# GpSimd forms the column units of a modulation matrix ahead, and the weight ring has seven slots, in a two-layer hybrid encoder

## Chip, cores, metric

One core of a Trainium2 chip runs the whole program in one launch. The metric is the device time in microseconds, median of the runs.

## What is computed

Two layers over x (512 tokens of 1024 channels, float32). Every layer first forms six modulation vectors from the conditioning vector c, then runs four groups of token mixers side by side and a mixture of 32 experts:

```python
ca = jax.nn.silu(c)
for l in range(DEPTH):
    mod = ca @ w_ada[l] + b_ada[l]
    sh1, sc1, gt1, sh2, sc2, gt2 = [m[:, None, :] for m in jnp.split(mod, 6, axis=-1)]
    h = rms_norm(x, g_norm1[l]) * (1.0 + sc1) + sh1
    proj = h @ w_in[l]
    # ya, yb, yc, yd: differential attention, neighbourhood attention, convolution, dilated attention
    mix = jnp.concatenate([ya, yb, yc, yd], axis=-1) @ w_out[l]
    x = x + gt1 * mix
    h2 = rms_norm(x, g_norm2[l]) * (1.0 + sc2) + sh2
    x = x + gt2 * hier_moe(h2, w_router_group[l], w_router_expert[l],
                           w_exp_gate[l], w_exp_up[l], w_exp_down[l])
return rms_norm(x, g_final)
```

w_ada is 1024 x 6144 per layer. Each of the 32 experts has three matrices of 2 MB; a token uses two experts of one group of eight.

## The kernel before

The weights come in units of 2 MB (128 partitions x 8 x 512; some are 1 MB) into a ring of six slots, loaded by SyncE in the order of the list ORDER. SyncE works strictly in that order: before each load it waits until the slot's earlier unit has been used. w_ada of a layer is twelve such units of 512 columns (u = 0 to 11): 0 and 1 are the first shift, 2 and 3 the first scale, 4 and 5 the first gate, 6 to 9 the second shift and scale, 10 and 11 the second gate.

- ADA_EARLY, the gates (4, 5, 10, 11): VectorE multiplies and adds them during the projections (early_product), TensorE sums over the partitions and spreads the result.
- ADA_LATER, the column units 6 to 9: in the attention, at steps 1, 9, 12 and 29 (ADA_STEPS). TensorE multiplies the silu vector with the unit (ada, L1041), which gives a row. VectorE turns it into columns (ada_turned, L1768), and two steps later (MOD_LAG) TensorE folds it (mod, L1059) and VectorE adds the bias (mod_out).
- ADA_NEXT, the units 0 to 3 of layer 1, are done in the same way in the routing of layer 0, between the last router logits and the first expert.

A layer goes through these stages. The projections go group by group, D, A, B, with q and k first, then v (product, L1015). In them VectorE rotates q and k and runs the 31 taps of the convolution over 2 x 128 channels (tap, L1793); the last 31 of 62 tap instructions stand in one piece ahead of B's first q and k. The attention has 32 units in 35 steps: D at 0 to 7, A at 8 to 23, B at 24 to 31. In a step i TensorE turns the probabilities of an earlier unit (turn, L1184), makes the scores of unit i (scores, L1170) and the output of another (attend, L1197 and L1210). VectorE takes maxima, ScalarE takes exponentials (expo, L1581 and L1584) and copies the turned probabilities out of PSUM (prob_out, L1598). Odd pairs are copied into z, the buffer of the convolution. So the first of these copies waits for conv_ready, which GpSimd gives when it has copied the convolution's result from z to yT (L930).

GpSimd's queue in a layer is: small loads (L917 to L921), those two copies, the bias tables of B's first two heads (L936 to L945, once D's last scores are used, since they lie over D's q and k), the tables of the other two (once A's last scores are used), six additions x += tmp in the output projection (L952), and then the gathers and scatters of the experts (L970, L980).

The output projection (out_part, L1228) is followed tile by tile by the transposes and logits of the router. Routing then ranks the tokens. In layer 1, which has no next units, idle_products (L1071) stand in the places of the row products.

The experts take their weights from nine places of 2 MB, three experts' worth: the six slots, home (a buffer used by nothing else), hT and work. BUF sets their order, await_first_free what the first load of each waits for (L843). After that each half place is loaded again as soon as TensorE has used it (expert_unit, L864). In layer 0 the order is home, then the places of the two w_out units, hT, the four slots of the ADA_NEXT units and work.

## Time and profile before

| | |
|---|---|
| median of 3 runs | 1806.28 us (1804.26 to 1807.28) |
| profiled execution | 1805.69 us |
| its span, first to last instruction | 1803.8 us |
| TensorE busy | 1589.4 us, 88% |
| VectorE, ScalarE, GpSimd busy | 39%, 24%, 11% |
| HBM | 520.99 MB read, 302 GB/s over the span |

Stages of the profiled execution, in us from the start of the span: layer 0 has its projections up to 208, the attention up to 312, the output projection up to 381, routing up to 411 and the experts up to 891. Layer 1 starts at 918, its attention at 1087, its output projection at 1192, routing at 1261, the experts at 1287, and they end at 1775. "Idle before" in a row is the time that the engine stood before the instruction, and behind the arrow stands what ended it. TensorE's counts are twice those of the program's text, since each float32 product is two records. L numbers are lines of the kernel above.

### The profile page before, as it was taken

The numbers are of one execution on the slowest core, as the hardware profiler recorded it, in microseconds if no ns is written. First come the engines' busy times: TensorE is split into PE (matmuls) and PEld (weight loads), VectorE is DVE, ScalarE is ACT, GpSimd is POOL, SyncE is SP. The second block draws the span as 40 slices with busy tenths as digits, with TensorE's granted clock in tenths as the row PEclk, the third lists the DMA queues.
The fourth block names the chain that finished last, engine by engine and source line by source line (L and its number), as shares of the span: only waits on it lengthen the run. The fifth ranks groups of instructions, "written<-read, shape, count | busy, mean of one in ns | idle before, by whom it ended". The sixth has DMA issues, their size and how long they took to land.

```text
span 1803.8 us, 22591 instructions
## 1 busy us (share of the span) xinstructions
PE 1589.4 (88%) x7494; PEld 763.4 (42%) x7494; DVE 695.3 (39%) x1432; ACT 435.6 (24%) x989; POOL 194.1 (11%) x199
## 2 busy tenths in 40 slices
PE   5999998998998998787889999999899988887883
PEld 2455645453333343333345555455333333333331
DVE  1677576352222112222157855743422222222124
ACT  2111567112111112111121016742111221111111
POOL 0000022111111011111000002101111111111010
PEclk9999999989999999999999999999999999999997
DMA  9625533079999999999972355212799999999994
GB/s 362 231 70 202 195 115 110 17 293 398 407 401 407 408 408 404 417 410 417 365 298 93 122 204 208 68 48 101 290 400 407 403 409 406 411 416 404 399 395 180
DMA packets 118493, 527.56 MB, mean 292 GB/s; under 512 B 16529, under 2 KB 22673, under 8 KB 69265
## 3 DMA queue, kind: packets, MB, share of 16 engines
q1 hardware_dynamic: 100944, 491.49, 69.0%
q0 software_dynamic: 12496, 24.51, 4.2%
q10 hardware_dynamic: 4976, 10.55, 1.6%
q8 instruction: 46, 0.75, 0.2%
q14 instruction: 31, 0.25, 0.0%
HBM read 520.99 MB, written 23.86 MB: 302 GB/s over the span
## 4 chain that ended last, share of the span: by engine, by line
PE 56%; DMA 27%; SPq 6%; DVE 5%; issue 3%; ACT 3%; POOL 1%; ACTq 0%; DVEq 0%; POOLq 0%
DMA ring<-in_w_exp_up 20%; PE ps L1015 18%; PE ps L1373 17%; PE ps L1228 6%; SPq L841 5%; PE ps L1371 4%; DMA hT<-in_w_exp_up 3%; PE ps L1170 2%; PE ps L1184 2%; PE ps L1210 2%; PE ps L1041 1%; DMA ring<-in_w_in 1%; ACT arena L1664 1%; DMA yexp_d<-arena,masks 1%; PE ps L1404 1%
## 5 line engine op out<-in xcount | busy, mean ns | idle before, releaser
L1373 PE MATMUL ps<-ring,arena 128*64 128x512 f32 x1952 | 589.1, 603 | 59.2 <-ACT arena L1664 35.0
L1373 PEld LDWEIGHTS ps<-ring,arena 128*64 128x64 f32 x1952 | 184.8, 138 | 273.5 <-issue 260.2
L1015 PE MATMUL ps<-ring,hT 128*128 128x512 f32 (+1 forms) x768 | 255.0, 487 | 1.5 <-DVE z L1804 0.9
L733 DVE TENSOR_TENSOR arena<-ps,arena 64x512 f32<-64x512 f32 (+1 forms) x64 | 44.3, 693 | 488.6 <-ACT arena L1658 418.6
L1658 ACT ACTIVATE arena<-ps 128x512 f32<-128x512 f32 x64 | 38.2, 597 | 778.9 <-PE ps L1373 724.3
L1015 PEld LDWEIGHTS ps<-ring,hT 128*128 128x128 f32 x768 | 144.4, 191 | 101.5 <-issue 91.2
L1373 PE MATMUL ps<-home,arena 128*64 128x512 f32 x320 | 148.6, 619 | 24.2 <-DMA ring<-in_w_exp_up 20.5
L1373 PE MATMUL ps<-hT,arena 128*64 128x512 f32 x336 | 151.5, 605 | 6.9 <-DMA ring<-in_w_exp_up 6.9
L980 POOL DMA_INDIRECT yexp_d<-arena,masks x64 | 59.3, 927 | 850.3 <-DVE arena L743 772.9
L741 DVE TENSOR_TENSOR arena<-ps,gate 64x512 f32<-64x512 f32 (+1 forms) x64 | 43.7, 683 | 266.2 <-PE ps L1373 246.6
L1228 PE MATMUL ps<-ring,hT 128*128 128x512 f32 x256 | 112.5, 595 | 0.0
L1650 ACT ACTIVATE arena<-ps,modc 128x128 f32<-128x128 f32 x256 | 96.5, 457 | 32.3 <-PE ps L1352 30.1
L1373 PEld LDWEIGHTS ps<-home,arena 128*64 128x64 f32 x320 | 44.6, 143 | 118.9 <-issue 116.9
L1793 DVE SCALAR_TENSOR_TENSOR work<-z,small,work 128x512 f32<-128x512 f32 x120 | 90.0, 751 | 3.9
L722 DVE TENSOR_SCALAR arena<-ps,modc 128x128 f32<-128x128 f32 x256 | 87.4, 403 | 5.9 <-PE ps L1352 2.3
L1373 PE MATMUL ps<-work,arena 128*64 128x512 f32 x320 | 73.1, 598 | 17.9 <-ACT arena L1664 17.9
L1352 PEld LDWEIGHTS ps<-cst,arena 128*128 128x128 f32 x512 | 62.2, 194 | 51.7 <-issue 51.7
L1352 PE MATMUL ps<-cst,arena 128*128 128x128 f32 x512 | 73.7, 287 | 2.4 <-DVEq L1759 2.4
L1170 PE MATMUL ps<-arena 64*128 64x512 f32 (+1 forms) x256 | 73.7, 655 | 0.0
L1228 PEld LDWEIGHTS ps<-ring,hT 128*128 128x128 f32 x256 | 47.8, 190 | 57.1 <-issue 57.1
L1373 PEld LDWEIGHTS ps<-hT,arena 128*64 128x64 f32 x336 | 45.8, 139 | 57.1 <-issue 56.0
L1404 PE MATMUL ps<-cst,arena 128*128 128x128 f32 x256 | 47.8, 309 | 23.9 <-DVE arena L733 23.7
(218 smaller groups left out, 1645.2 us busy)
## 6 DMA issues: line engine op xcount, KB each, us to landing
ring<-in_w_exp_up SPq DMA_DIRECT2D x108, 1024.0 KB
ring<-in_w_exp_down SPq DMA_DIRECT2D x88, 1024.0 KB
ring<-in_w_exp_gate SPq DMA_DIRECT2D x62, 1024.0 KB
ring<-in_w_ada SPq DMA_DIRECT2D x24, 2048.0 KB, 11.1
home<-in_w_exp_gate SPq DMA_DIRECT2D x44, 1024.0 KB
work<-in_w_exp_down SPq DMA_DIRECT2D x40, 1024.0 KB
hT<-in_w_exp_gate SPq DMA_DIRECT2D x22, 1024.0 KB
hT<-in_w_exp_up SPq DMA_DIRECT2D x20, 1024.0 KB
```

The source lines that it names most:

```text
L722: last = dve.tensor_scalar(xgT[j][:, k, :], ps[:, 4, P * q:P * q + P], modc[:, 3, k:k + 1], modc[:, 2, k:k + 1], ALU.mult, ALU.add)
L841: sp.dma_start(places[b][:, n * h:n * h + n], flat[i % SPAN][e][:, n * h:n * h + n]).then_inc(half_in[h][b], 16)
L980: pool.indirect_dma_start(yexp_d[l], bass.IndirectOffsetOnAxis(ap=lst[0:w, e:e + 1], axis=0), yexp[e % 2][0:w, :], None, bounds_check=last ...
L1015: last = pe.matmul(out, lhs(k), rhs(k), start=(k == 0), stop=(k == n - 1))
L1170: fills(pe.matmul(bank(key), qkT[g][p0:p0 + n, hp, P * t:P * t + P], qkT[g][p0:p0 + n, 2 + hp, :], start=True, stop=True, tile_position=(p ...
L1228: last = pe.matmul(bank(key), yT[:, k, P * t:P * t + P], slot(unit)[:, k, :], start=(k == K_OUT[0]), stop=(k == K_OUT[-1]))
L1352: last = pe.transpose(bank_e(b).rearrange("p (a s) -> p a s", a=4)[:, q, :], xg[j][:, k:D:KD], ident)
L1371: last = [pe.matmul(outs[c], lhs(k), rhs(c, k), start=(k == 0), stop=(k == n - 1)) for c in range(2)]
L1373: last = [pe.matmul(outs[c][HALF * c:HALF * c + HALF, :], lhs(k)[:, 0:HALF], rhs(c, k), start=(k == 0), stop=(k == n - 1), tile_position=( ...
L1404: last = pe.transpose(ps[:, 2, P * c:P * c + P], hid[j][:, c:DE:KE], ident)
L1650: last = act.activation(xgT[j][:, q, :], ps[:, 3, P * q:P * q + P], ACT.Identity, scale=modc[:, 3, q:q + 1], bias=modc[:, 2, q:q + 1])
L1793: ins = dve.scalar_tensor_tensor(conv[f], z[:, f, k:k + S], w, conv[f], ALU.mult, ALU.add)
```

## The change

Three things.

1. ADA_LATER and ADA_NEXT units are formed on GpSimd (column_sums): one multiplication of the whole unit, in its ring slot, by the silu vector, and three instructions that add its eight parts to one. TensorE then sums over the partitions with eight products of a single column (mod_of_sums), and VectorE adds the bias as before. The row product, its turning and its copy are gone for these units; units 0 to 3 of layer 0 stay as they were.
2. Places: GpSimd does the four later units ahead of the copies of the convolution, the first unit of layer 1 behind them, two more between the two pairs of bias tables, and the last behind the tables. TensorE's sums stand at steps 4, 8, 10, 12 (later) and 16, 23, 27 and output tile 2 (next). Routing has none left, and its idle products now run in both layers.
3. home is gone and the ring has seven slots. The experts still have nine places; in layer 0 the five slots of the last later unit and the four next units come first, then w_out's two, hT and work.

```diff
-SLOTS = 6
+SLOTS = 7
-ADA_STEPS = [1, 9, 12, 29]
+LATER_STEPS, NEXT_STEPS, NEXT_TILE = [4, 8, 10, 12], [16, 23, 27], 2
-MOD_LAG = 2
+def mods_at(l, step):
+    later = [ADA_LATER[l][n] for n, s in enumerate(LATER_STEPS) if s == step]
+    return later + [unit for unit, s in zip(ADA_NEXT[l], NEXT_STEPS) if s == step]
...
-        order += [("ada",) + item for item in ADA_LATER[l]]
+        order += [("ada",) + item for item in ADA_LATER[l] + ADA_NEXT[l][:1]]
         order += [("wout", l, n) for n in range(2)]
-        order += [("ada",) + item for item in ADA_NEXT[l]]
+        order += [("ada",) + item for item in ADA_NEXT[l][1:]]
...
         if ADA_NEXT[l]:
-            last = [HOME] + late[0:2] + [FEATURES] + late[2:6] + [WORK]
-        else:
-            last = [HOME] + late + [FEATURES, WORK]
+            late = late[0:2] + late[4:] + late[2:4]
+        last = late + [FEATURES, WORK]
...
-        home = sb("home", [P, KD, 512])
...
-                if old is not None:
+                if old is not None and ORDER[old][0] == "ada" and ORDER[old][1:] in ADA_EARLY[l]:
+                    sp.wait_ge(early_ready, len(ADA_EARLY[l]) * l + ADA_EARLY[l].index(ORDER[old][1:]) + 1)
+                elif old is not None:
                     await_filled(sp, last_use(old))
...
                     if b == WORK:
                         sp.wait_ge(slots_ready, 2 * l + 2)
-                        if not ADA_NEXT[l]:
-                            sp.wait_ge(xg_in[0], 16 * (l * HE + 1))
-                        for m, u in ADA_NEXT[l][-1:]:
-                            await_filled(sp, (m, "mod", u))
+                        sp.wait_ge(xg_in[0], 16 * (l * HE + 1))
...
+                def column_sums(m, u):
+                    unit = UNIT["ada", m, u]
+                    await_unit(pool, unit)
+                    w = slot(unit)
+                    link(pool.tensor_tensor(w, w, view(csil, 0, [[KD, P], [1, KD], [0, 512]]), ALU.mult))
+                    for n in (4, 2):
+                        link(pool.tensor_tensor(w[:, 0:n, :], w[:, 0:n, :], w[:, n:2 * n, :], ALU.add))
+                    pool.tensor_tensor(w[:, 0, :], w[:, 0, :], w[:, 1, :], ALU.add).then_inc(sums_ready, 1)
+                pool.wait_ge(silu_ready, 1)
+                for m, u in ADA_LATER[l]:
+                    column_sums(m, u)
                 await_filled(pool, (l, "v", "B", TT - 1))
                 for f in range(2):
                     pool.wait_ge(conv_silu, 2 * l + f + 1)
                     pool.tensor_copy(yT[:, FIRST_F["C"] + f, :], z[:, f, HALO:HALO + S]).then_inc(conv_ready, 1)
+                for m, u in ADA_NEXT[l][:1]:
+                    column_sums(m, u)
                 for hp in range(2):
...
+                    for m, u in ADA_NEXT[l][1 + 2 * hp:3 + 2 * hp]:
+                        column_sums(m, u)
...
+            def mod_of_sums(l, u):
+                key, w, p0 = (l, "mod", u), slot(UNIT["ada", l, u]), HALF * (u % 2)
+                pe.wait_ge(sums_ready, sums_before(l, u) + 1)
+                await_free(pe, key)
+                for k in range(KD):
+                    last = pe.matmul(bank(key)[p0:p0 + HALF, k:k + 1], w[:, 0, k:512:KD], C["ones"],
+                                     start=True, stop=True, tile_position=(0, p0))
+                fills(last, key)
...
-                    if ada_at(l, i - MOD_LAG) is not None:
-                        n = ada_at(l, i - MOD_LAG)
-                        mod(*ADA_LATER[l][n], n % 2)
+                    for m, u in mods_at(l, i):
+                        mod_of_sums(m, u)
                     for u in closed_at(i):
                         attend(u)
-                    if ada_at(l, i) is not None:
-                        ada(*ADA_LATER[l][ada_at(l, i)])
```

On TensorE this is the start of layer 0's attention before, from the scores of the first two steps on; L1041 is the row product of step 1, L1059 its fold at step 3:

```order
49 L1170 MATMUL ps<-arena 128x512 x4
50 L1041 MATMUL ps<-ring,csil 32x512 x8
51 L1184 MATMUL ps<-cst,work 128x128 x8
52 L1170 MATMUL ps<-arena 128x512 x2
53 L1184 MATMUL ps<-cst,work 128x128 x8
54 L1170 MATMUL ps<-arena 128x512 x2
55 L1059 MATMUL ps<-work,cst 32x8 x2
56 L1197 MATMUL ps<-cst,rinv 64x128 x2
57 L1210 MATMUL ps<-work,arena 64x128 x8
```

And now, where L1055 is the new sum over the partitions (the other lines are the same instructions, moved by ten or eleven lines of text):

```order
49 L1181 MATMUL ps<-arena 128x512 x4
50 L1195 MATMUL ps<-cst,work 128x128 x8
51 L1181 MATMUL ps<-arena 128x512 x2
52 L1195 MATMUL ps<-cst,work 128x128 x8
53 L1181 MATMUL ps<-arena 128x512 x2
54 L1208 MATMUL ps<-cst,rinv 64x128 x2
55 L1221 MATMUL ps<-work,arena 64x128 x8
56 L1195 MATMUL ps<-cst,work 128x128 x8
57 L1181 MATMUL ps<-arena 128x512 x2
58 L1055 MATMUL ps<-cst,ring 64x1 x8
```

The row product has gone from step 1, and one step behind the place of its fold, at step 4, stand eight products of one column, read from the ring.

On GpSimd the queue of layer 0 before, from the last small load to the first tables:

```order
13 L921 DMA masks<-in_dilation 128x896
14 L930 COPY hT<-z 128x512 [waits bank_filled2,conv_silu,table_in,params_in]
15 L930 COPY hT<-z 128x512 [waits conv_silu]
16 L936 DMA arena<-in_rpb 64x896 [waits bank_drained3]
17 L936 DMA arena<-in_rpb 64x896 x3
```

And now (rows 19 to 30 are three more units like rows 15 to 18):

```order
15 L919 TENSOR_TENSOR ring<-ring,csil 128x4096 [waits silu_ready,slot_in1,table_in,params_in]
16 L921 TENSOR_TENSOR ring<-ring 128x2048 [waits pool_chain]
17 L921 TENSOR_TENSOR ring<-ring 128x1024 [waits pool_chain]
18 L922 TENSOR_TENSOR ring<-ring 128x512 [waits pool_chain]
...
31 L930 COPY hT<-z 128x512 [waits conv_silu,bank_filled2]
32 L930 COPY hT<-z 128x512 [waits conv_silu]
33 L919 TENSOR_TENSOR ring<-ring,csil 128x4096 [waits slot_in5]
...
37 L938 DMA arena<-in_rpb 64x896 [waits bank_drained3]
...
43 L919 TENSOR_TENSOR ring<-ring,csil 128x4096 [waits slot_in1]
...
51 L938 DMA arena<-in_rpb 64x896 [waits bank_drained3]
```

The copies and both pairs of tables now stand behind whole units, and each unit behind the load of its slot.

## Rows read from the trace of the kernel before

**Rows 1.** Stage windows: stretch, length, busy and instructions of PE, PEld, DVE, ACT, POOL, clock, DMA, GB/s

```profile
411.00:891.00 480.00, 419.15 (x1892) 173.46 (x1892) 105.92 (x217) 83.95 (x187) 55.54 (x59) 0.99 1.01 406
1287.00:1775.00 488.00, 416.38 (x1912) 169.45 (x1912) 107.16 (x218) 86.13 (x190) 56.40 (x60) 0.98 0.98 392
312.00:381.00 69.00, 68.92 (x265) 36.33 (x266) 22.05 (x34) 12.73 (x26) 7.54 (x6) 1.00 0.21 78
```

**Rows 2.** The page's part 4, chain of waits by line, share of the span

```profile
DMA ring<-in_w_exp_up 20%; PE ps L1015 18%; PE ps L1373 17%; PE ps L1228 6%; SPq L841 5%; PE ps L1371 4%; DMA hT<-in_w_exp_up 3%; PE ps L1170 2%; PE ps L1184 2%; PE ps L1210 2%; PE ps L1041 1%; DMA ring<-in_w_in 1%; ACT arena L1664 1%; DMA yexp_d<-arena,masks 1%; PE ps L1404 1%
```

**Rows 3.** TensorE in the attention: timeline (start, us), then windows of 5 us

```profile
209.16 1.92 PE L1041 MATMUL ps<-ring,csil 128*32 128x512 f32 x16
247.63 3.64 PE L1041 MATMUL ps<-ring,csil 128*32 128x512 f32 x16
...
240.00:245.00 5.00, 3.66 (x36) 1.00 0.80 270
245.00:250.00 5.00, 4.82 (x20) 0.59 0.41 155
```

**Rows 4.** Timeline of TensorE, from the last logits to the first expert, both layers

```profile
381.16 3.66 PE L1015 MATMUL ps<-arena,hT 128*128 128x36 f32 x32
...
392.22 3.55 PE L1064 MATMUL ps<-cst,work 128*64 128x1 f32 x32
...
411.24 1.08 PE L1373 MATMUL ps<-home,arena 128*64 128x512 f32 x1 [1.81 <-ACT arena L1650]
...
1260.62 3.66 PE L1015 MATMUL ps<-arena,hT 128*128 128x36 f32 x32
...
1287.02 0.61 PE L1373 MATMUL ps<-home,arena 128*64 128x512 f32 x1 [1.81 <-issue]
```

**Rows 5.** Timeline of ScalarE in layer 0's attention: first copy to z, exponentials of steps

```profile
215.71 1.06 ACT L1598 ACTIVATE z<-ps 128x512 f32<-128x512 f32 x2
...
234.31 0.69 ACT L1581 ACTIVATE work<-ps,masks 128x512 f32<-128x512 f32 x1 [0.96 <-DVE masks L1901]
...
263.29 0.69 ACT L1581 ACTIVATE arena<-ps,masks 128x512 f32<-128x512 f32 x1
...
265.74 0.69 ACT L1581 ACTIVATE work<-ps,masks 128x512 f32<-128x512 f32 x1 [0.52 <-DVE masks L1901]
```

**Rows 6.** Groups of GpSimd by form: busy, mean ns, idle before

```profile
L952 POOL TENSOR_TENSOR x<-x,work 128x512 f32<-128x512 f32 x12 | 15.1, 1265 | 118.8 <-DVE work L1998 118.8
L945 POOL TENSOR_TENSOR arena<-arena,cst 128x896 f32<-128x896 f32 x8 | 14.3, 1787 | 0.7
```

**Rows 7.** Timeline of SyncE's queue, and a load's median from issue to landing

```profile
144.65 30.54 SPq L796 DMA_DIRECT2D ring<-in_w_ada  x4
...
ring<-in_w_out SPq DMA_DIRECT2D x4, 2048.0 KB, 7.8
```

**Rows 8.** Timeline of GpSimd in layer 0's attention

```profile
208.49 0.61 POOL L930 COPY hT<-z 128x512 f32<-128x512 f32 x1 [0.32 <-ACT z L1567]
231.60 2.12 POOL L936 DMA_DIRECT2D arena<-in_rpb  x4 [22.50 <-DVE masks L1914]
...
281.95 2.17 POOL L936 DMA_DIRECT2D arena<-in_rpb  x4 [35.17 <-ACT work L1581]
...
295.15 1.77 POOL L945 TENSOR_TENSOR arena<-arena,cst 128x896 f32<-128x896 f32 x1
```

**Rows 9.** Windows up to 13 us behind the first expert, layers 0 and 1

```profile
361.00:424.00 63.00, 55.85 (x315) 31.36 (x313) 30.45 (x115) 13.16 (x26) 7.07 (x6) 0.86 0.83 319
1237.00:1300.00 63.00, 55.54 (x257) 31.12 (x257) 27.78 (x105) 12.08 (x24) 7.67 (x7) 0.97 0.60 220
```

**Rows 10.** Timelines: VectorE's taps; GpSimd's and VectorE's instructions that overlap

```profile
145.35 24.24 DVE L1793 SCALAR_TENSOR_TENSOR work<-z,small,work 128x512 f32<-128x512 f32 x31
...
238.01 2.46 POOL L944 TENSOR_SCALAR arena<-arena 128x896 f32<-128x896 f32 x1 [4.29 <-DMA arena<-in_rpb]
...
240.01 0.75 DVE L1932 SCALAR_TENSOR_TENSOR work<-work,coef 128x512 f32<-128x512 f32 x1
```

More of the change, by code:

```diff
@@ L115, with sums_before @@
 ADA_NEXT = [[(l + 1, u) for u in range(NORM1_UNITS) if l + 1 < DEPTH] for l in range(DEPTH)]
-def ada_at(l, step):
-    return ADA_STEPS.index(step) if step in ADA_STEPS else None
+def mods_at(l, step):
+    later = [ADA_LATER[l][n] for n, s in enumerate(LATER_STEPS) if s == step]
+    return later + [unit for unit, s in zip(ADA_NEXT[l], NEXT_STEPS) if s == step]
+def sums_before(m, u):
+    order = [unit for l in range(DEPTH) for unit in ADA_LATER[l] + ADA_NEXT[l]]
+    return order.index((m, u))
 def unit_order():
@@ L153, in plan_buffers @@
         else:
-            left = [last[n] for n in (6, 7, 1, 4, 2, 5, 0, 3, 8)]
-            order = [b for b in left if b < SLOTS]
+            order = [last[n] for n in (6, 7, 8, 0, 1, 3, 4, 2, 5) if last[n] < SLOTS]
         ring.append({n: order[i % SLOTS] for i, n in enumerate(ATT[l])})
@@ L253, in plan_banks @@
         for step in range(NSTEP):
-            if ada_at(l, step - MOD_LAG) is not None:
-                m, u = ADA_LATER[l][ada_at(l, step - MOD_LAG)]
+            for m, u in mods_at(l, step):
                 take((m, "mod", u), 7)
@@ L261, in plan_banks @@
                     take((l, "meanA", f), (7, 3)[f])
-            if ada_at(l, step) is not None:
-                m, u = ADA_LATER[l][ada_at(l, step)]
-                take((m, "ada", u), 7)
         for t in range(TT + 1):
@@ L270, in plan_banks @@
                 take((l, "router_shift"), 7)
+            if t == NEXT_TILE:
+                for m, u in ADA_NEXT[l][len(NEXT_STEPS):]:
+                    take((m, "mod", u), 7)
             if t:
@@ L497, in last_use @@
             if kind == "ada":
-                return l, "mod" if (l, u) in ADA_EARLY[l] else "ada", u
+                return l, "ada" if l == 0 and u < NORM1_UNITS else "mod", u
             if kind == "win":
@@ L843, in await_first_free @@
                 def await_first_free(b):
-                    if b == HOME and l:
-                        i = BUF[l - 1].index(b)
-                        await_expert_used(l - 1, max(e for e in range(NE) if e % SPAN == i // SPAN), i % SPAN)
                     if b < SLOTS:
@@ L1050, in mod @@
                 await_free(pe, key)
-                if u // 2 % 3 == 2:
-                    fills(pe.matmul(bank(key), ones, tmp[:, part, :], start=True, stop=True), key)
-                    return
                 p0 = HALF * (u % 2)
@@ L1287, in _ @@
                         logits(t - 2)
-                half = NORM1_UNITS // 2
-                for m, u in ADA_NEXT[l][:half]:
-                    ada(m, u)
-                if not ADA_NEXT[l]:
-                    await_drained(pe, (l, "out", TT - 2, 1))
-                    idle_products(5, 1)
+                await_drained(pe, (l, "out", TT - 2, 1))
+                idle_products(5, 1)
                 key = (l, "rank")
@@ L1301, in _ @@
                 fills(pe.matmul(bank(key)[:, 0:n], C["before"], hots5, start=False, stop=True), key)
[L1302 to L1306 removed]
+                idle_products(2, 1)
                 key = (l, "list_parts")
@@ L1317, in _ @@
                 fills(pe.matmul(bank(key)[:, 0:NE], list_parts, C["fold32"], start=True, stop=True), key)
-                for m, u in ADA_NEXT[l][half:]:
-                    ada(m, u)
-                if not ADA_NEXT[l]:
-                    idle_products(3, 1)
+                idle_products(3, 1)
                 key = (l, "more_lists")
```

65 lines of the change are left out of this document (19 added, 46 removed).

## Prediction

> **What bounds the kernel now.** I read the stage windows first. The two expert loops take 480 and 488 of 1803.8 us, with the DMA engines busy all the time (1.01 and 0.98, 406 and 392 GB/s), while TensorE is busy for 419 and 416 us of them [rows 1]. Outside them TensorE sets the pace: in the output projection of layer 0 it is busy for 68.92 of 69 us. The chain of waits says the same: expert weights on one side, projections (L1015), experts (L1373) and output (L1228) on the other [rows 2]. So a gain must either start the weight stream with more bytes in hand, or take time from TensorE in the stages between. A loss comes where something else becomes last.
>
> **TensorE's side of the change.** A row product (L1041) of one unit takes 1.92 us, and 3.64 us where the clock is low [rows 3]. What replaces it, eight pairs of a 64-column weight load and a one-column product, is in the trace too: L1064, two units in 3.55 us, 1.8 us each [rows 4]. So TensorE gets nearly nothing back per unit. What it gets is the way out of a bad place: of the steps from 234.31 to 263.29 in the attention of layer 0 there are eight, which at the pitch of the steps behind them (263.29 to 265.74, 2.45 us) would take 19.6 us and take 29.0 [rows 5]. Two row products, their turning on VectorE, a wait and a stretch at a granted clock of 0.59, the 2.4 GHz level falling to 1.2 after a stretch in which TensorE was busy for 3.66 of 5 us [rows 3], lie in these 9.4 us. I take all of it as saved and put 3 x 1.8 = 5.3 us for the new sums at steps 8, 10, 12 in its place. The product at step 29 with its small sum saves 2.2, the new one at step 4 costs 1.8. Layer 1 has the same pattern.
>
> **GpSimd's side.** One unit is 4096 products, then 2048, 1024 and 512 additions per partition. The product has an operand that is repeated, as L945 has: 1787/896 = 1.99 ns an element, 8.2 us. The additions are like L952: 1265/512 = 2.47 ns, 8.9 us. Together 17.0 us a unit [rows 6]. Bounds from the same two rows: a line through both (1.36 ns an element and 0.57 us an instruction) gives 12.7 us, all at 2.47 ns gives 19.0. I take 17.0, since each form is priced by its nearest row.
>
> **Where that is late.** SyncE can issue the first of these units only behind w_in's last piece, at 144.65 [rows 7]. That piece (1 MB, 2.6 us at 406 GB/s) and then a load like w_out's (7.8 us) bring it in at 155.0. Four units take GpSimd to 223.0. Only then does it reach the two copies of the convolution (L930, 0.61 us each), and these are queued behind on GpSimd: done at 224.2 instead of 209.1 [rows 8]. ScalarE waits for them before it writes the second pair's probabilities into z, which it does at 215.71 [rows 5]. So the attention stands still from there: +8.5 us, in both layers. (In this the product saved at step 1 is used up already.) After such a stand TensorE starts at the low clock; going by the 5 us at 0.59, some 3 us a layer. Sum for **layer 1**: 8.5 + 3 + 1.8 + 5.3 - 9.4 - 2.2 = **+7.0 us**.
>
> Layer 0 has more. GpSimd's queue goes on: the unit of layer 1 (+17.0, to 241), the bias tables of the first heads, two more units, then the tables of the last heads. Tables take 15.0 us from their first issue (281.95 to 296.92 [rows 8]), and the second ones stand on the path: the last group's scores wait for them. The first tables wait for D's scores, before at 231.60 [rows 8], now at 231.6 + 8.5 + 3 + 1.8 = 244.9; then 259.9, 276.9, 293.9. By its own steps the attention would be there at 281.95 + 8.5 + 3 + 1.8 + 5.3 - 9.4 + 1.8 (step 16) = 293.0. The later counts: 293.9, **+12.0 us**. The sums at steps 23 and 27 lie in that wait. Step 29 gives -2.2, the sum at output tile 2 costs +1.8 on a full TensorE [rows 1]. From the last logits to the first expert layer 0 needs 411.24 - 384.82 = 26.4 us and layer 1, without column units there, 1287.02 - 1264.28 = 22.7: -3.7 [rows 4].
>
> **The weight stream.** Five places of layer 0 now free during attention against one before, 8.4 MB, which at 406 GB/s looks like 20.7 us. But nine places are all there are. Layer 1 already has this pattern, five places loaded early. In the 63 us up to 13 us behind the first expert it moved 220 x 63 = 13.9 MB on top of 10.5; layer 0 moved 319 x 63 = 20.1 on top of 2.1 [rows 9]. It has 24.4 against 22.2 MB in hand, not 8.4 more: the DMA engines idle while the places are full. So **-5.4 us** (2.2 MB). Layer 0 in all: 12.0 - 2.2 + 1.8 - 3.7 - 5.4 = **+2.5 us**.
>
> At nothing I put the ring's seventh slot in the projections (TensorE is the bound there, and the place home was SBUF too), the loads that wait for early_sum_ready instead of a bank, and ScalarE's and VectorE's copies that go: TensorE covers them, up to about 2 us a layer if I am wrong.
>
> The profiled execution took 1805.69 us (span 1803.8), 0.6 under the median of the three runs shown. 1805.7 + 7.0 + 2.5 = **1815 us**.
>
> **VectorE beside GpSimd.** From 145.35 VectorE runs 31 taps of the convolution (L1793), each with two SBUF inputs, to 169.6 [rows 10], and the new products fall into that. Does one hold the other out? In the trace GpSimd ran a tensor_scalar from 238.01 for 2.46 us, and VectorE began L1932, two SBUF inputs, in it at 240.01 and took 0.75 us, as always [rows 10]; no row shows a two-input instruction of VectorE begun inside a two-input one of GpSimd. So the sum has no term for it. The Trainium skill says otherwise (SBUF — State Buffer, section on the two separate sides): the port pair that both share is an exclusive lock, held for the whole instruction, against a VectorE instruction with two SBUF inputs. By that rule the row at 240.01 could not stand as it does, but the rows don't reach the new case. That is a rival of its own, with two sizes.
>
> **Rivals.**
> - *GpSimd is cheap* (other side: faster). It decides at (215.7 - 1.2 - 155.0)/4 = 14.9 us a unit: below it no one waits for GpSimd. Then layer 1 gives -1.9 (step 1) + 1.8 + 5.3 - 9.4 - 2.2 = -6.4, layer 0 -2.4 up to the tables, -2.2 + 1.8 - 3.7 - 5.4 behind: -11.9. Time 1787. For it: the line through two rows gives 12.7. Against: both forms singly give more. Chance 0.17.
> - *All 8.4 MB count*: 15 us less, 1800. Against it stands layer 1, whose loop is no shorter than layer 0's. 0.05.
> - *Costs and gains cancel* (a unit of some 16 us, no fall of the clock): 1802 to 1810. 0.12.
> - *Taps first*: GpSimd gets through only when the taps end at 169.6, 14.6 us later in each layer: 1815 + 29 = 1844. 0.15.
> - *GpSimd first*: VectorE gets one tap in per GpSimd instruction. 18.7 taps are left at 155.0, 16 instructions let 16 by, the last tap ends at about 238, 68 us late; TensorE has three banks, some 10 us of work, in hand: about +58 a layer in place of the 11.5 of stand and clock, 1815 + 93 = 1908. 0.08.
> - My forecast, 1810 to 1836 with a unit at up to 19 us: 0.43.
>
> **The numbers.** Faster is 0.17 + 0.05 = 0.22, same 0.12, slower 0.43 + 0.15 + 0.08 = 0.66 (0.2%, 3.6 us, is about what a measurement of this kernel can tell from no change). The range goes from the first rival's time to the fourth's: 1786 to 1848. Outside lie the last rival and a little at either end.
>
> **What would show it.** L919 at 8 to 9 us and a unit at 17; L930 done near 224 and 1104 with ScalarE's first write to z right behind; both bias tables' releases by GpSimd; step pitch of 2.45 us without the low clock at 245; DMA share under 0.8 in the 30 us before the first expert of layer 0. Wrong would be: a unit under 15 us, or taps longer than 0.78 us or with gaps.

## The result, and the profile after

| | before | after |
|---|---|---|
| median | 1805.59 us (1804.26 to 1807.28, 4 runs) | 1960.46 us (1959.91 to 1962.12, 4 runs) |
| span of the profiled execution | 1803.8 us | 1958.1 us |
| mean granted clock of TensorE | 0.973 | 0.934 |

The ratio is 1.0866, 95% interval 1.0853 to 1.0879: 155 us slower. I had forecast 1815 us, 1786 to 1848. The direction was right, the size was not.

Stages first, from TensorE's timeline (first scores, first output product, first expert):

| stage, us | before | after | difference |
|---|---|---|---|
| layer 0: start to first scores | 207.2 | 262.2 | +55.0 |
| layer 0: attention | 106.1 | 153.4 | +47.3 |
| layer 0: output projection and routing | 97.9 | 95.9 | -2.0 |
| first expert of layer 0 to first scores of layer 1 | 676.1 | 727.9 | +51.8 |
| layer 1: attention | 105.4 | 110.4 | +5.0 |
| layer 1: output projection and routing | 94.2 | 93.1 | -1.1 |
| first expert of layer 1 to the end | 516.8 | 515.2 | -1.6 |

So nearly all of it lies in three stretches: the projections of both layers and the attention of layer 0. The windows of after have the columns of [rows 1]; the last one holds the first 105 of the 110 us of layer 1's attention:

```profile
262.00:415.00 153.00, 121.33 (x858) 77.75 (x858) 99.48 (x176) 78.81 (x199) 84.88 (x34) 0.77 0.36 123
...
511.00:995.00 484.00, 421.74 (x1914) 175.09 (x1914) 108.02 (x221) 86.08 (x190) 56.58 (x60) 0.99 1.00 403
1239.00:1344.00 105.00, 94.64 (x764) 59.80 (x764) 68.47 (x164) 73.35 (x188) 22.24 (x18) 0.93 0.35 119
```

The expert loop of layer 0 is as before (484 us at 403 GB/s; it was 480 at 406). The attention of layer 0 ran at a granted clock of 0.77. The page's chain by line, against [rows 2], has three new names: the sums over the partitions, L1055, in place of the row product, and two of VectorE's, the taps, now L1779, and the coefficient of the mixture, L1916.

```profile
PE ps L1369 17%; DMA ring<-in_w_exp_up 14%; PE ps L1019 14%; DVE work L1779 8%; DMA hT<-in_w_exp_up 6%; PE ps L1239 6%; SPq L833 5%; PE ps L1367 3%; PE ps L1181 3%; PE ps L1195 2%; PE ps L1221 2%; DMA ring<-in_w_in 1%; PE ps L1055 1%; ACT arena L1650 1%; DVE coef L1916 1%
```

**The projections.** The taps' group of the page (busy, mean ns, idle before), and then their line in the view of one source line (ns min/median/max, first and last start):

```profile
L1779 DVE SCALAR_TENSOR_TENSOR work<-z,small,work 128x512 f32<-128x512 f32 x120 | 198.7, 1657 | 3.9
```

```profile
L1779 DVE SCALAR_TENSOR_TENSOR work<-z,small,work x120: 737/752/7389, 101.4 to 1200.2; 128x512 f32<-128x512 f32 x120
```

The median of a tap is what it was, 752 ns, but the longest took 7389. Before, none took more than 753. The 31 taps of [rows 10], 24.24 us, take 78.61 from 145.61. Here are five of them in the chain of waits in order of time (start, us, what), and then GpSimd's timeline:

```profile
155.84 0.76 DVE work L1779
...
156.63 7.40 DVE work L1779
...
164.05 4.89 DVE work L1779
...
168.97 2.73 DVE work L1779
...
171.72 1.65 DVE work L1779
```

```profile
156.04 7.43 POOL L919 TENSOR_TENSOR ring<-ring,csil 128x4096 f32<-128x4096 f32 x1 [117.95 <-DMA ring<-in_w_ada]
163.55 7.59 POOL L921 TENSOR_TENSOR ring<-ring 128x2048 f32<-128x2048 f32 x2
171.21 1.59 POOL L922 TENSOR_TENSOR ring<-ring 128x512 f32<-128x512 f32 x1
```

Each tap is as long as the instruction of GpSimd beside it: 7.4 for the product, 4.9 and 2.7 for the first two additions, 1.65 for the third. That repeats four times, with the four units, until 223. The taps are not slower, they start and then stand. TensorE has worked off by 173.3 all that does not need VectorE's later results, and stands:

```profile
225.96 2.05 PE L1139 MATMUL ps<-arena,cst 128*128 128x512 f32 x2 [52.66 <-DVEq L1745]
...
1202.69 2.05 PE L1139 MATMUL ps<-arena,cst 128*128 128x512 f32 x2 [52.67 <-DVEq L1745]
```

**The attention of layer 0.** GpSimd forms all four units of layer 1 there. Beside the first (264 to 279.5) VectorE runs nothing with two SBUF inputs, and nothing there is stretched. The next two (304 to 336) meet VectorE's coefficient (L1916, one element a partition) and mixture (L1918), both with two SBUF inputs. The last, from 393.6, meets an addition (L1932) that takes 5.73 us in place of 1.20, and TensorE stands for 4.53. VectorE's timeline beside the second unit, and TensorE's waits for it there and beside the third:

```profile
304.99 6.25 DVE L1916 SCALAR_TENSOR_TENSOR coef<-masks,neglam,rinv 128x1 f32<-128x1 f32 x1
311.28 5.07 DVE L1918 SCALAR_TENSOR_TENSOR work<-work,coef 128x512 f32<-128x512 f32 x1
```

```profile
316.40 1.12 PE L1195 MATMUL ps<-cst,work 128*128 128x128 f32 x4 [13.21 <-DVE work L1918]
...
334.91 1.11 PE L1195 MATMUL ps<-cst,work 128*128 128x128 f32 x4 [7.99 <-DVE work L1918]
```

An instruction on one element, 0.22 us elsewhere, takes 6.25 us. And TensorE's clock pays for the waits also when they are over (windows of TensorE alone: busy, clock, DMA share, GB/s):

```profile
310.00:340.00 30.00, 15.61 (x66) 0.50 0.19 70
340.00:360.00 20.00, 20.00 (x94) 0.50 0.29 106
```

From 340 to 360 nothing keeps TensorE waiting, and it works all of the 20 us at the 1.2 GHz level.

### The profile page after: what moved, and what is told of

Its sections match the earlier page's. It is cut to its first block, busy times and chain, and to the rows that moved or that the text cites. A ratio compares the mean times of both kernels' runs of the same rounds, so it can differ in the third digit from the quotient of the medians.

```text
span 1958.1 us, 22475 instructions
## 1 busy us (share of the span) xinstructions
PE 1613.2 (82%) x7446; PEld 790.8 (40%) x7446; DVE 830.6 (42%) x1412; ACT 437.1 (22%) x987; POOL 388.7 (20%) x247
## 4 chain that ended last, share of the span: by engine, by line
PE 51%; DMA 23%; DVE 14%; SPq 6%; issue 3%; ACT 3%; POOL 1%; DVEq 0%; ACTq 0%; POOLq 0%
PE ps L1369 17%; DMA ring<-in_w_exp_up 14%; PE ps L1019 14%; DVE work L1779 8%; DMA hT<-in_w_exp_up 6%; PE ps L1239 6%; SPq L833 5%; PE ps L1367 3%; PE ps L1181 3%; PE ps L1195 2%; PE ps L1221 2%; DMA ring<-in_w_in 1%; PE ps L1055 1%; ACT arena L1650 1%; DVE coef L1916 1%
## 5 line engine op out<-in xcount | busy, mean ns | idle before, releaser
L1369 PEld LDWEIGHTS ps<-ring,arena 128*64 128x64 f32 x2288 | 192.6, 138 | 450.3 <-issue 421.0
L1779 DVE SCALAR_TENSOR_TENSOR work<-z,small,work 128x512 f32<-128x512 f32 x120 | 198.7, 1657 | 3.9
L1369 PE MATMUL ps<-hT,arena 128*64 128x512 f32 x320 | 146.1, 611 | 0.0
L919 POOL TENSOR_TENSOR ring<-ring,csil 128x4096 f32<-128x4096 f32 x12 | 88.0, 7336 | 228.6 <-DMA ring<-in_w_ada 228.6
L1139 PE MATMUL ps<-arena,cst 128*128 128x512 f32 x16 | 10.4, 735 | 105.5 <-DVEq L1745 105.3
L921 POOL TENSOR_TENSOR ring<-ring 128x2048 f32<-128x2048 f32 (+1 forms) x24 | 88.6, 3693 | 1.9
L1181 PE MATMUL ps<-arena 64*128 64x512 f32 (+1 forms) x256 | 83.0, 731 | 0.6 <-ACT arena L1549 0.6
L1195 PE MATMUL ps<-cst,work 128*128 128x128 f32 x296 | 48.0, 303 | 33.8 <-DVE work L1918 26.5
L1348 PE MATMUL ps<-cst,arena 128*128 128x128 f32 x512 | 73.6, 287 | 0.0
```

What stands on the lines that cost most here:

```text
L919: link(pool.tensor_tensor(w, w, view(csil, 0, [[KD, P], [1, KD], [0, 512]]), ALU.mult))
L921: link(pool.tensor_tensor(w[:, 0:n, :], w[:, 0:n, :], w[:, n:2 * n, :], ALU.add))
L1181: fills(pe.matmul(bank(key), qkT[g][p0:p0 + n, hp, P * t:P * t + P], qkT[g][p0:p0 + n, 2 + hp, :], start=True, stop=True, tile_position=(p ...
L1195: last = pe.transpose(bank4(key)[:, kt, :], src[:, P * kt:P * kt + P], ident)
L1348: last = pe.transpose(bank_e(b).rearrange("p (a s) -> p a s", a=4)[:, q, :], xg[j][:, k:D:KD], ident)
L1369: last = [pe.matmul(outs[c][HALF * c:HALF * c + HALF, :], lhs(k)[:, 0:HALF], rhs(c, k), start=(k == 0), stop=(k == n - 1), tile_position=( ...
```

## The experiments

**Theory A**: an instruction of GpSimd with two SBUF inputs holds VectorE's instructions with two SBUF inputs out for its whole length, and VectorE gets one in between two of them. **Rivals**: B, the ring, the new order or TensorE's new sums cost the time; C, both engines share bandwidth; D, TensorE's clock falls because the row products are gone; E, every instruction of GpSimd that reads SBUF holds.

### 1. The sums left out, all or by halves

```diff
 def column_sums(m, u):
     unit = UNIT["ada", m, u]
     await_unit(pool, unit)
     w = slot(unit)
+    if True:                    # later_only: (m, u) in ADA_NEXT[0]; next_only: not in ADA_NEXT[0]
+        pool.tensor_tensor(w[:, 0, 0:8], w[:, 0, 0:8], w[:, 1, 0:8], ALU.add).then_inc(sums_ready, 1)
+        return
```

> The changed kernel with the ring of seven, the early loads and TensorE's short products, but GpSimd does one addition of 8 elements a unit in place of the product and the three additions: the products with the modulation weights are left out, so the later columns' values are not computed. Theory A (GpSimd's two-input instructions hold VectorE out of its two-input instructions): all 155 us come from them, so this runs under the kernel before, by the terms that my prediction gave to the rest (row products gone, routing 3.7, weight stream 5.4): 1785 to 1797 us, the 31 taps of 145 us take 24.2 us again. Rival B (the ring, the other order of loads or the missing products cost the time): over 1900 us.

> As no_sums, but the eight units that their own layer uses (four at the projections of each layer) are multiplied and added in full; those of layer 1 ahead are left out. Theory A: the delays of the projections alone return, 54.5 us in layer 0 and about 48.7 in layer 1, on a rest of about 1790: 1880 to 1900 us, the taps' longest instruction 7.4 us. Rival C (the loss is spread over both kinds of unit by what they add to SBUF's traffic, eight to four): about 1790 + 2/3 of 170 = 1903, and no tap as long as a GpSimd instruction. Rival B: as the changed kernel, 1950 or more in both halves.

> As no_sums, but only the four units of layer 1 that are taken ahead in layer 0 are multiplied and added; the eight later units of the layers are left out. Theory A: only the attention of layer 0 is longer, by at most the 48 us that it grew in the changed kernel, on a rest of about 1790: 1825 to 1840 us; taps 0.75 us each in both layers; attention of layer 1 as before. Rival C: 1790 + 1/3 of 170 = 1847 with the time spread. Rival D (TensorE's clock fell because of the row products' absence, not of the waits): no_sums too is over 1830, with the clock at 0.5 in the attention.

| | median, us | ratio (95%) | first scores, layer 0 | attention 0 | attention 1 |
|---|---|---|---|---|---|
| before | 1804.35 | | 207.2 | 106.1 | 105.4 |
| no_sums | 1828.86 | 1.0135 (1.0116 to 1.0153) | 206.4 | 122.4 | 114.1 |
| later_only | 1934.33 | 1.0721 (1.0690 to 1.0752) | 261.5 | 126.0 | 114.0 |
| next_only | 1853.02 | 1.0275 (1.0258 to 1.0292) | 207.3 | 149.1 | 110.2 |
| after | 1960.46 | 1.0866 (1.0853 to 1.0879) | 262.2 | 153.4 | 110.4 |

The parts add up: the eight later units cost 1934.3 - 1828.9 = 105.5 us, the four ahead 1853.0 - 1828.9 = 24.2, together 129.6, against 1960.5 - 1828.9 = 131.6 for both. The later units cost it in the projections, the others in the attention of layer 0, as A has it. None of the three kernels computes all the modulation columns, but the way from the first expert of layer 0 to the next scores is 677.5 us in no_sums and 676.3 in next_only against 676.1 before, so their stages can be compared. Taps in no_sums and next_only stay at 24.24 us for the 31, at most 754 ns each in next_only.

But all three missed A's ranges: no_sums 1785 to 1797, later_only 1880 to 1900 and next_only 1825 to 1840. The last two missed by what no_sums did, since their ranges stood on a rest of 1790 us where 1829 was measured. With next to no work on GpSimd the change still loses 24.5 us, and 16.3 + 8.7 = 25.0 lie in the two attentions. Two windows over the attention of layer 0, first of before, then of no_sums (columns of [rows 1]):

```profile
207.00:313.00 106.00, 98.03 (x830) 55.72 (x830) 70.08 (x180) 77.24 (x199) 22.48 (x18) 0.97 0.37 125
```

```profile
206.00:329.00 123.00, 113.84 (x868) 73.84 (x867) 71.57 (x176) 78.58 (x200) 23.02 (x22) 0.88 0.45 153
```

TensorE is busy for 15.8 us more, at a clock of 0.88 in place of 0.97. Clock: (1 - 0.88) x 123 - (1 - 0.97) x 106 = 11.6 us. Work: seven sums in no_sums take 14.58 us of TensorE (L1058, 2.1 each), the four row products and four folds of before took 9.41 + 0.94; +4.2. In layer 1, counted alike (114 us at 0.88, 106 at 0.97), the clock costs 13.7 - 3.2 = 10.5 and the four sums, 8.33 us against 9.03 + 0.94, save 1.6. These are figures of one execution, which took 1831.3 us where the four runs go from 1826.0 to 1832.2, so they are good to a few us. The lost clock is what rival D names, which I had as an aside of next_only; its mark, no_sums over 1830, was missed by 1 us.

### 2. A row product put back, its result thrown away

```diff
 await_free(pe, key)
+if (l, u) in ADA_LATER[l][2:]:
+    for r in range(2):
+        for q in range(4):
+            pe.matmul(bank(key)[32 * q:32 * q + 32, :], view(csil, 4 * r + q, ...), w[:, 4 * r + q, :], ...)
 for k in range(KD):
```

> As no_sums (the sums of GpSimd left out), but TensorE computes a row product with the unit's weights ahead of the small sums of steps 10 and 12 of both attentions and throws it away: work without a result, of the form that the kernel before had at steps 9 and 12. Theory D (with the row products the attention lost the dense work that brought the clock back after the stretch of little work at 240 us; no_sums stood at a granted clock of 0.50 to 0.66 from 250 to 280 us, where the kernel before had 0.80 and 0.86 in 240 to 260 and then 1.00): the clock is back by 262 us, the attention of layer 0 takes 106 to 112 us in place of 122.4 and that of layer 1 105 to 109 in place of 114.1, the whole 1806 to 1817. Rival F (the clock stays low for the waits themselves, whatever TensorE computes): the attentions are 2 x 1.9 to 2 x 3.6 us longer than in no_sums, the whole 1833 to 1843.

Measured: 1821.63 us (1819.89 to 1824.16), ratio 1.0095 (1.0080 to 1.0111), 7 us under no_sums though it does 4 products more. The attentions took 116.3 and 109.1 us in place of 122.4 and 114.1, which is some 6 and 5 of the 16 and 9 us, where 106 to 112 and 105 to 109 were expected. The total lies between the two ranges on record, 1806 to 1817 for D and 1833 to 1843 for F, and nearer to D's. How long the low level lasts shows in windows of TensorE. Before:

```profile
248.00:250.00 2.00, 2.00 (x12) 0.50 0.00 0
250.00:252.00 2.00, 2.00 (x12) 0.50 0.00 0
252.00:254.00 2.00, 2.00 (x14) 0.81 0.50 125
254.00:256.00 2.00, 2.00 (x24) 1.00 1.03 393
```

no_sums, one window of 20 us:

```profile
248.00:268.00 20.00, 19.08 (x89) 0.51 0.41 152
```

no_sums_fill:

```profile
252.00:254.00 2.00, 2.00 (x16) 0.50 0.19 70
254.00:256.00 2.00, 2.00 (x16) 0.85 0.00 0
256.00:258.00 2.00, 2.00 (x15) 1.00 0.19 33
258.00:260.00 2.00, 2.00 (x16) 0.50 0.88 287
260.00:262.00 2.00, 2.00 (x18) 0.64 0.98 414
```

In all three the clock falls where TensorE waited for VectorE. With a row product in the low stretch (before at 247.63 [rows 3], no_sums_fill at 251.22) the high level is back some 5 and 3 us after that product began (by the means of the windows, at 252.8 and 254.6). Without one TensorE works on small products, busy for 19.08 of 20 us, and stays at 1.2 GHz. The low stretch is shorter, and so is the attention. The stage window of no_sums_fill (columns of [rows 1]) goes beside the two in experiment 1:

```profile
207.00:323.00 116.00, 107.07 (x897) 68.25 (x893) 72.26 (x176) 77.79 (x199) 22.84 (x22) 0.97 0.47 162
```

The clock is that of before, 0.97 against no_sums' 0.88, and in layer 1 it is the same pair. What keeps the attentions 10.2 and 3.7 us over those of before is TensorE's work: the sums take 14.57 and 8.32 us and the two row products 5.50 and 5.12, where before it was 9.41 and 9.03 of row products and 0.94 of folds, so 9.7 and 3.5 us more.

That the row products bring the clock back is the reading that fits all three, but it isn't shown alone, as TensorE also stood for less ahead of the low stretch (1.72 us in no_sums_fill, 2.86 in no_sums). A rival was not tested either: the sums of one column might be what lowers the clock. It falls again, without a stand, behind the sum at 254.72 of no_sums_fill and behind that at 269.87 of no_sums. With two row products beside them the same sums leave the mean clock at 0.97, but no kernel here runs without row products and without these sums.

### 3. Which forms hold which

> The kernel before, with four instructions of GpSimd of 2048 elements in turn beside the 31 taps of layer 0 that start at 145.4 us: an addition of two inputs, a multiplication by a constant of one input, a copy and a fill. Theory A: one tap lasts as long as the addition (4.8 us), one starts every time the port comes free, and beside the other three the taps stay at 0.75 us, so that the run of 31 taps is 24.2 + about 4 us. Rival E (every GpSimd instruction that uses SBUF holds VectorE out): taps as long as the copy and the fill too (some 2 to 6 us each), 24.2 + 12 or more. Rival C (bandwidth shared): every tap beside any of the four is stretched in some proportion, none to the length of the GpSimd instruction.

```diff
+pool.wait_ge(rot_ready, NQK * l + 2 * TT)
+link(pool.tensor_tensor(spot[:, 0:2048], spot[:, 0:2048], spot[:, 2048:4096], ALU.add))
+link(pool.tensor_scalar(spot[:, 0:2048], spot[:, 0:2048], 1.0, None, ALU.mult))
+link(pool.tensor_copy(spot[:, 0:2048], spot[:, 2048:4096]))
+pool.memset(spot[:, 0:2048], 0.0).then_inc(probe_done, 1)
```

GpSimd's timeline, then the chain of waits over the taps (L1804 there):

```profile
144.54 4.86 POOL L934 TENSOR_TENSOR home<-home 128x2048 f32<-128x2048 f32 x1 [106.32 <-DVE work L1901]
149.50 5.69 POOL L935 TENSOR_SCALAR home<-home 128x2048 f32<-128x2048 f32 x1
155.26 2.07 POOL L936 COPY home<-home 128x2048 f32<-128x2048 f32 x1
157.39 1.80 POOL L937 MEMSET home<- 128x2048 f32 x1
```

```profile
145.06 4.90 DVE work L1804
...
149.99 4.03 DVE work L1804
...
155.62 2.27 DVE work L1804
157.91 0.76 DVE work L1804
```

The whole took 1810.81 us, and the 31 taps 33.15, which is 8.9 more. One tap lasts as long as the addition, one is held for 3.3 of the multiplication's 5.7 us (two of 0.75 follow while it still runs), one for the whole copy, none by the fill. So A was too narrow in GpSimd's forms, and E too wide by the second half of the multiplication. The other side of the question:

> The kernel before, with sixteen additions of two inputs and 1024 elements (about 2.6 us each, 41 us in all) on GpSimd from 145.4 us in layer 0, and three times seven instructions of 512 elements on VectorE beside them, ahead of the 31 taps: an addition and a product of two SBUF inputs, a copy and a multiplication of one SBUF input, an addition and a scalar_tensor_tensor of one PSUM and one SBUF input, a copy out of PSUM. Theory A (only VectorE's instructions with two SBUF inputs are held): six of the 21 last as long as GpSimd's, about 2.6 us, and the other fifteen 0.3 to 0.8 us as ever. Rival E (all that read SBUF are held): eighteen of them at about 2.6 us, only the copy out of PSUM short. Rival C (bandwidth): all a little longer, none at 2.6.

The diff is of the same kind: sixteen additions of 1024 elements on GpSimd, seven forms three times on VectorE. The kernel also puts B's first q and k tile in another place, so its whole time (6775 us, of which 5602 lie between the first expert of layer 0 and the next scores) is that of another computation, and only the stretch up to 200 us is read. GpSimd's additions took 39.93 us from 145.93, 2.5 each. VectorE's timeline beside them, then one round after their end:

```profile
178.73 2.44 DVE L1880 COPY home<-home 128x512 f32<-128x512 f32 x1
181.21 2.44 DVE L1881 TENSOR_SCALAR home<-home,small 128x512 f32<-128x512 f32 x1
183.69 0.69 DVE L1882 TENSOR_TENSOR home<-ps,home 128x512 f32<-128x512 f32 x1
184.41 1.99 DVE L1883 TENSOR_TENSOR home<-home 128x512 f32<-128x512 f32 x1
186.44 0.75 DVE L1884 SCALAR_TENSOR_TENSOR home<-ps,small,home 128x512 f32<-128x512 f32 x1
...
187.95 0.69 DVE L1879 TENSOR_TENSOR home<-home 128x512 f32<-128x512 f32 x1
188.68 0.43 DVE L1880 COPY home<-home 128x512 f32<-128x512 f32 x1
189.14 0.49 DVE L1881 TENSOR_SCALAR home<-home,small 128x512 f32<-128x512 f32 x1
```

Two of the three rounds, 14 instructions, fall beside the additions, the third behind them. Held are the four forms that read SBUF alone, also the copy (2.44 against 0.43 us) and the multiplication by a column (2.44 against 0.49), eight of the 14; the three with a PSUM input are not, though two of them read SBUF too. A had two forms held and E six; neither had four. The Trainium skill (SBUF — State Buffer, section on the two separate sides) gives this division: VectorE takes the port pair it shares with GpSimd with two SBUF inputs or in a two-port mode, which a float32 copy from SBUF to SBUF triggers. The 0.43 us of the copy against 0.69 out of PSUM agree.

> The kernel before, with other forms on GpSimd from 145.4 us in layer 0: eight multiplications by a constant and eight copies of 1024 elements with one SBUF input, four fills of 2048 with none, and one addition. Beside them VectorE runs twenty pairs of an addition (two SBUF inputs, 0.69 us alone) and a copy (one, 0.43 us alone) of 512 elements, ahead of the 31 taps. Rule E (any GpSimd instruction that reads SBUF holds VectorE's SBUF-to-SBUF instructions out, also copies, as probe_vector had it; a fill does not): one VectorE instruction in about 2 to 3 us beside the multiplications, one in about 1 us beside the copies, 0.69 and 0.43 us beside the fills. Theory A as first stated (only GpSimd's two-input forms hold): 0.69 and 0.43 us beside all but the last addition. A mixed outcome, as the 4.0 us tap beside the 5.7 us multiplication of probe_forms hints: held for part of each multiplication, some 0.7 of its length.

The whole took 1840.89 us. Eight one-input multiplications of 1024 elements took 24.62 us from 144.96 (3.1 each), eight copies 10.42 (1.3), four fills 7.55. Beside a multiplication one instruction of VectorE in four or so is late, by 0.7 us; beside the copies every one is, and beside the fills, where VectorE was at its taps from 180.5 on, none. Two lines of each of the first two stretches:

```profile
151.38 1.41 DVE L1879 TENSOR_TENSOR home<-home 128x512 f32<-128x512 f32 x1
152.82 0.43 DVE L1880 COPY home<-home 128x512 f32<-128x512 f32 x1
...
177.76 1.40 DVE L1879 TENSOR_TENSOR home<-home 128x512 f32<-128x512 f32 x1
179.20 1.15 DVE L1880 COPY home<-home 128x512 f32<-128x512 f32 x1
```

It is the mixed outcome: copies hold for their whole length, a multiplication by a constant for part of it (0.7 of 3.1 us here, 3.3 of 5.7 in probe_forms). The Trainium skill (SBUF — State Buffer, the same section) has the pair held for the whole instruction; for this form the runs show less, and the runs decide.

### 4. How long, and in which order

> The changed kernel with each product and each addition of GpSimd cut into instructions of 512 elements: 15 a unit in place of 4, the same sums. Theory A1 (VectorE gets one instruction in for each instruction of GpSimd, whatever their length): the 31 taps need 31 of GpSimd's instructions, two units, and end near 190 us in place of 224; the projections of each layer come some 30 us earlier, and the attention of layer 0 loses less: 1880 to 1910 us. Theory A2 (the port is held for as long as GpSimd has work, and one VectorE instruction slips in only at waits): taps to 224, 1955 or more. Rival C (bandwidth shared by time): no difference, 1960.

```diff
-link(pool.tensor_tensor(w, w, view(csil, 0, [[KD, P], [1, KD], [0, 512]]), ALU.mult))
+for k in range(KD):
+    last = pool.tensor_tensor(w[:, k, :], w[:, k, :], view(csil, k, [[KD, P], [0, 512]]), ALU.mult)
+link(last)
```

(and the additions alike.) Measured: **1865.26 us** (1862.33 to 1869.02), ratio 1.0334 (1.0317 to 1.0351): the same sums, in 15 instructions in place of 4, take back 95 of the 155 us. GpSimd's first unit beside the taps and the taps:

```profile
155.43 11.39 POOL L920 TENSOR_TENSOR ring<-ring,csil 128x512 f32<-128x512 f32 x8 [117.61 <-DMA ring<-in_w_ada]
166.90 9.95 POOL L924 TENSOR_TENSOR ring<-ring 128x512 f32<-128x512 f32 x6
```

```profile
144.82 37.14 DVE L1783 SCALAR_TENSOR_TENSOR work<-z,small,work 128x512 f32<-128x512 f32 x31
```

13 taps are done at 155, 18 are left, and they get through beside about 17 instructions of GpSimd, at 182 us. One for one is A1; it was even better than the 190 us expected, since not all 31 taps were left, and the whole lies under A1's 1880 to 1910. A2, which had 1955 or more, and C, which had 1960, are out.

> The split kernel with pieces of 256 elements, 30 instructions of GpSimd a unit. Theory A1 (VectorE gets one instruction in for each instruction of GpSimd): 18 taps beside it now take some 1.0 us each in place of 1.5, so the projections end 6 to 10 us earlier in each layer and the attention's held instructions shorten; but a unit is longer by the fixed part of each instruction, some 20 us in place of 17, which the bias tables feel: 1845 to 1865 us. Rival G (what is left of the loss is not the length of GpSimd's instructions): no earlier end of the projections, 1865 to 1885.

Measured: 1887.68 us (1880.71 to 1889.35), ratio 1.0456 (1.0426 to 1.0485), slower than split, and outside both ranges, A1's 1845 to 1865 and G's 1865 to 1885. The taps did what A1 says: 31 in 28.43 us, first scores at 212.0 (split 219.8). But the attentions took 148.6 and 138.2 us in place of 132.7 and 117.7. ScalarE's waits there (total, times, longest):

```profile
ACT z L1599 <- POOL hT L936: 22.2, 1, 22.2
```

That is the wait which my forecast was built on: the copies of the convolution behind four units on GpSimd, done at 242.6 here. It shows only where the taps are not the later ones.

> The changed kernel, but GpSimd begins a layer's four later units only when the convolution's last tap is done. Theory A: the taps take 24.2 us as before and the projections end at 207; four units run from about 170 to 237 and the copies of the convolution follow at 238, so ScalarE's first write to z stands 22 us in each layer, and VectorE's two-input instructions of the attention up to 237 are held too: the attention of layer 0 at 160 to 175 us, of layer 1 at 125 to 145; the whole 1880 to 1915 us, 45 to 80 under the changed kernel. Rival C (traffic alone): the same work has to be moved, 1950 or more.

```diff
 pool.wait_ge(silu_ready, 1)
+for f in range(2):
+    pool.wait_ge(conv_done[f], l + 1)
 for m, u in ADA_LATER[l]:
```

Measured: 1889.59 us (1887.40 to 1892.09), ratio 1.0466 (1.0448 to 1.0482), inside A's 1880 to 1915: taps 751 ns on the mean, first scores at 212.1, the attentions 164.1 and 126.9 us. TensorE does nothing from 270 to 280 there, while L1918 (the coefficient, in that kernel's lines) takes 6.25 us again. The same work of GpSimd, moved behind the taps, costs half as much and still 84 us.

> The split kernel (pieces of 512 elements) with the row product of no_sums_fill ahead of the small sums of steps 10 and 12 in both attentions. If the low clock behind the stretch of little work is a loss of its own, as no_sums_fill against no_sums has it (7 us in all), 1855 to 1862 us against 1865 for split. If the waits for VectorE keep TensorE slow whatever it computes, 1866 to 1875.

Measured: 1870.00 us (1868.08 to 1874.77), ratio 1.0373 (1.0352 to 1.0395), 5 us over split: attention 0 took 136.2 us against 132.7, attention 1 115.4 against 117.7, and the way to it 2.9 more. That is inside the range of the theory that the waits keep TensorE slow, 1866 to 1875. The gain of no_sums_fill does not carry over to a kernel in which TensorE still waits for VectorE.

### 5. The ring by itself

> The kernel before with the ring of seven places in place of six and the place home, and nothing else: row products on TensorE, the order of the loads and the steps as before. Theory A: the ring costs nothing and brings nothing, within 4 us of the kernel before. Rival B (the seventh place, or the experts' other order of places, costs time in the expert loops): 1810 or more, longer between first expert and end.

The diff is that of the ring alone: SLOTS = 7, home gone from BUF. Measured: 1805.28 us (1799.56 to 1806.96, 11 runs), ratio 0.9995 (0.9985 to 1.0004). The seventh slot is worth nothing and costs nothing. Of B the new order of the loads is out by no_sums, which has it and loses in the attentions alone; TensorE's new sums stay in, as part of the 24.5 us of experiment 1.

## Why the prediction was wrong

**The step that failed** is the one in "VectorE beside GpSimd": "So the sum has no term for it." It stood beside L1932 beginning inside a GpSimd instruction at 240.01 and taking 0.75 us [rows 10], and beside the remark that no row shows the new case. So the term was put at nothing without a row for it. The instruction beside it was a multiplication by a constant, and L1932 began 2.0 us into its 2.46. Such an instruction lets go of the port before its end: in probe_forms the held tap was done at 154.02, so it got the port 1.9 us before the multiplication ended at 155.19. A row of the wrong form, met in its last fifth, stood where a term of 105.5 us beside the taps and 24.2 beside the attention was missing. The rule of the Trainium skill (SBUF — State Buffer, the two separate sides), which the text gave a rival, was right for the form in question: a tap beside GpSimd's product took 7.40 us, the product 7.43.

Point by point:

- **A unit takes 17.0 us on GpSimd**: 16.7 in the trace (product 7.4, additions 4.8, 2.6 and 1.3 to 1.6), well inside 12.7 to 19.0. Two errors offset each other in part: the product was forecast at 8.2, the additions at 8.9, which took 9.3. The first started at 156.04, forecast 155.0; four were done at 223.0, forecast 223.0.
- **The copies of the convolution are late and ScalarE stands 8.5 us a layer**: not in after, since the projections themselves ended at 262. The step was right as a mechanism, as split256 shows with a wait of 22.2 us.
- **All 9.4 us of eight steps are saved once the row products leave**: wrong, and with the other sign. no_sums shows the attentions 16.3 and 8.7 us longer than before. The low clock in those steps was not the row products' doing; by experiment 2 they rather shortened it. The eight steps themselves, which I had at 29.0 - 9.4 + 5.3 = 24.9 us with their three sums, took 36.6 and 36.9 us in no_sums. The part of the change that is not on GpSimd costs 24.5 us in all, where my terms for it (those of the rival "GpSimd is cheap") gave 18.3 of gain.
- **TensorE gets nothing back per unit**: right. A sum took 2.1 us, 1.8 forecast.
- **Routing gains 3.7 us**: right. From the last output product to the first expert it is 29.3 us in no_sums and 29.2 in after, against 33.5: -4.2. Output tile 2 cost 2.2 of it.
- **The weight stream gives 5.4 us**: no. The expert loop of layer 0 is no shorter (484 us at 403 GB/s), and in ring7 and no_sums the way from the first expert to the next scores is 0.7 and 1.3 us longer. The 2.2 MB in hand bought nothing.
- **The rivals.** "GpSimd first" was what happened in the projections: +58 us a layer forecast, 55.0 and 51.8 measured (TensorE's wait is 52.7 in each). The nearness is partly luck. I had added the taps' own 14.6 us to GpSimd's 68, but they ran inside it, and the last tap ended at 224.2, not 238. And TensorE had 1.9 us in hand behind the taps' old end, not 10: it stood from 173.3, where it went on at 172.88 before. Its total of 1908 fell 52 short, as it had neither the units beside the attention's coefficient, mixture and addition (24 us by next_only) nor the lost clock, and kept the gains above. I had given it 0.08 and put it outside the range.

In sum the 155 us are: 105.5 for the later units beside the taps, 24.2 for the units ahead beside the attention, 24.5 for the rest of the change, nearly all in the attentions, which have lost the row products and gained the sums (about 22 of them clock, 3 TensorE's work; what lowers the clock there is not shown singly).

No version here beats the kernel before. Even with GpSimd's work free, no_sums_fill stands 16 us over it, and the new sums save TensorE nothing.

## What to carry to other kernels

An engine that has nothing to do is free only if its port is too: before float32 work goes to GpSimd, list VectorE's SBUF-to-SBUF instructions in that stretch, and count one of them for each GpSimd instruction that reads SBUF, as long as that one. If both must run, short pieces help by themselves (15 in place of 4 gave 95 us back), down to where the fixed part of each piece delays what is queued behind (the convolution's copies were done at 233.3 in split and at 242.6 in split256, which was 22 us slower). And a dense product on TensorE right behind a wait may be worth its time for the clock (7 us in no_sums_fill, nothing in split_fill): look at what stands there before taking it away.

## What the runs showed of the hardware that I had not expected

- GpSimd against VectorE in float32: an addition or a product of two inputs and a copy held VectorE out for their whole length (up to 7.4 us, even an instruction on one element); a multiplication by a constant for 0.7 of 3.1 us or 3.3 of 5.7, counted from where VectorE's instruction began; a fill did not hold the taps at all.
- On VectorE it strikes instructions whose tensors are all in SBUF, with one input (copy 2.44 in place of 0.43 us) as with two. One PSUM input sets it free: 0.69 and 0.75 us beside GpSimd's additions.
- GpSimd pays too: a product of 512 elements took 11.39 / 8 = 1.42 us beside taps, 8.47 / 8 = 1.06 without.
- TensorE stayed at 1.2 GHz for 20 us of no_sums in which it was busy for 19.08 with small products; in the two kernels with a row product in such a stretch it was back some 5 and 3 us after that product's start. All kernels that lack row products have the sums of one column in their place, so which of the two keeps the clock low is open.
